# Keys and values of the prompt memory as split products in a decoder step on one core

## The reference

```python
def memory_kv(mem, g, wk, wv):
    m = rms_norm(mem, g)                       # (1, 256, 1024)
    k = (m @ wk).reshape(B, M, XA_HEADS, XA_HEAD_DIM)
    v = (m @ wv).reshape(B, M, XA_HEADS, XA_HEAD_DIM)
    return k, v                                # both are outputs, too

def mixing(x, ...):
    z = rms_norm(x, g) @ w_in
    ...
    y_pool, pool_state = multiscale_pool(u_pool, ...)
    c, conv_state = causal_conv(u_rnn, ...)
    hs, hT = rg_lru(c, ...)
    y_rnn = hs * gelu(u_gate)
    merged = concatenate([rms_norm(y_pool, g_pool), rms_norm(y_rnn, g_rnn)])
    return merged @ w_out                      # "x1" in the kernel
```

## Time and profile before

| what | value |
|---|---|
| median of the three runs | 1110.73 us (1109.42 to 1127.9) |
| the profiled execution | 1109.17 us, span 1107.4 us |
| TensorE busy | 1061.4 us, 96% of the span |
| VectorE, ScalarE, GpSimd busy | 748.3, 646.5, 262.8 us (68%, 58%, 24%) |
| chain of work that ended last | TensorE 90%, DMA 3%, VectorE 3%, ScalarE 2% |
| keys and values on that chain (line 1659) | 5% |
| mean granted TensorE clock | 0.982 of full speed |

### The profile page before, as it was taken

The page is one execution under the profiler, slowest core; times in us unless marked ns, Lnnn a source line. Parts: engine busy times, 40 slices in busy tenths (PEclk is TensorE's granted clock), DMA queues, the critical chain, the costliest instruction groups (busy, mean ns, idle before and its releaser), DMA issues.

```text
span 1107.4 us, 17623 instructions
## 1 busy us (share of the span) xinstructions
PE 1061.4 (96%) x5991; PEld 796.5 (72%) x5991; DVE 748.3 (68%) x1332; ACT 646.5 (58%) x850; POOL 262.8 (24%) x180
## 2 busy tenths in 40 slices
PE   5999999999999999999999999999999999999991
PEld 5999458999669888666667666766667666766660
DVE  4733834633934575787788777887788778887762
ACT  4374343432643313677767776677767776677662
POOL 1001320000000101233333333333333333333321
PEclk8999999999999899999999999999999999999996
DMA  9500336050953525899999999999999999999945
GB/s 300 225 4 31 142 143 229 1 229 27 379 211 157 227 79 192 288 359 375 368 367 369 368 377 363 351 357 357 364 366 369 359 356 358 369 367 374 361 113 172
DMA packets 64342, 299.02 MB, mean 270 GB/s; under 512 B 12591, under 2 KB 15227, under 8 KB 39718
## 3 DMA queue, kind: packets, MB, share of 16 engines
q1 hardware_dynamic: 49102, 261.93, 61.7%
q0 software_dynamic: 15200, 36.55, 13.4%
HBM read 281.34 MB, written 34.00 MB: 285 GB/s over the span
## 4 chain that ended last, share of the span: by engine, by line
PE 90%; DMA 3%; DVE 3%; ACT 2%; SPq 1%; issue 1%; POOLq 0%; ACTq 0%; DVEq 0%
PE pair L1920 23%; PE pair L181 18%; PE pair L1954 16%; PE pair L1933 10%; PE pair L1659 5%; PE pair L1905 5%; PE pair L1562 3%; PE pair L1940 1%; DMA regA<-in_w_in 1%; PE pS L1868 1%; PE pair L1752 1%; PE pair L1760 1%; PE pS L1731 1%; DMA acc_rows<-regL 1%; DMA regL<-h_rows,regL 1%; DVE regL L1113 1%
## 5 line engine op out<-in xcount | busy, mean ns | idle before, releaser
L1920 PE MATMUL pair<-w_hi,h_parts 128*96 128x512 f32 x768 | 267.7, 430 | 0.0
L715 POOL DMA_INDIRECT acc_rows<-regL x64 | 93.0, 1453 | 389.8 <-ACT regL L1032 275.2
L1920 PEld LDWEIGHTS pair<-w_hi,h_parts 128*96 128x96 f32 x768 | 121.5, 165 | 69.7 <-issue 33.9
L1954 PE MATMUL pair<-w_hi,act_parts 128*96 128x512 f32 x512 | 165.0, 404 | 2.6 <-DVE act_parts L1509 2.6
L706 POOL DMA_INDIRECT regL<-h_rows,regL x65 | 139.7, 2148 | 74.7 <-DVE regL L1351 49.4
L1032 ACT ACTIVATE regL<-pair,regL 96x1024 f32<-96x1024 f32 x64 | 71.1, 1110 | 125.0 <-PE pair L1954 125.0
L1455 DVE TENSOR_TENSOR lo_A<-regA,w_hi 128x1536 fp32r<-128x1536 f32 x64 | 111.9, 1749 | 0.2 <-ACT w_hi L992 0.2
L1954 PEld LDWEIGHTS pair<-w_hi,act_parts 128*96 128x96 f32 x512 | 80.2, 167 | 29.9 <-issue 2.8
L992 ACT CAST w_hi<-regA 128x1536 fp32r<-128x1536 f32 x64 | 94.7, 1482 | 0.0
L1505 DVE TENSOR_TENSOR lo_B<-regB,w_hi 128x2048 fp32r<-128x2048 f32 x32 | 73.4, 2293 | 29.6 <-ACT w_hi L1027 29.6
L1505 DVE TENSOR_TENSOR lo_A<-regA,w_hi 128x2048 fp32r<-128x2048 f32 x32 | 73.4, 2292 | 24.7 <-ACT w_hi L1027 24.7
(11 more groups left out here) (344 smaller groups left out, 2207.3 us busy)
## 6 DMA issues: line engine op xcount, KB each, us to landing
regA<-in_exp_w_gate SPq DMA_DIRECT2D x32, 1024.0 KB, 9.1
regA<-in_exp_w_up SPq DMA_DIRECT2D x32, 1024.0 KB, 12.2
regA<-in_exp_w_down SPq DMA_DIRECT2D x32, 1024.0 KB, 14.0
regB<-in_exp_w_down SPq DMA_DIRECT2D x32, 1024.0 KB, 15.3
regB<-in_exp_w_gate SPq DMA_DIRECT2D x16, 1024.0 KB, 10.0
regB<-in_exp_w_up SPq DMA_DIRECT2D x16, 1024.0 KB, 13.6
regC<-in_exp_w_gate SPq DMA_DIRECT2D x16, 1024.0 KB, 9.2
regC<-in_exp_w_up SPq DMA_DIRECT2D x16, 1024.0 KB, 12.6
```

The lines of the kernel that those rows point to most:

```text
L715: pool.indirect_dma_start(acc_rows, bass.IndirectOffsetOnAxis(ap=kept[0:SLOTS, r, 0:1].bitcast(U32), axis=0), yX[r][0:SLOTS, :], None, bou ...
L1920: ins = pe.matmul(out, x, w, start=False, stop=half == 1 and k == CUT_K - 1 and s == 2, skip_group_check=True)
L1954: ins = pe.matmul(pair[2][0:SLOTS, h, :], act_parts[:, x, k, :], w[:, k, cols], start=k == 0 and s == 0, stop=k == KF - 1 and s == 2)
```

## The change

The keys and values become split products. ScalarE's mT copies now write the rounded part (`mT_hi`), and VectorE, after its polynomial for softplus, makes the rest (`leave_mT`) and is now the one that sets the pair free. The weights of K and V are cut in chunks of 128 rows by 1024 columns: `cut_kv(n)` on ScalarE and `leave_kv(n)` on VectorE, n = 0 to 7 for K and 8 to 15 for V. Rounded parts rotate through five places for K and three for V (`KV_PLACE`), the rests overwrite the weights. `kv` goes over the chunks outermost and serves both token tiles with each, so K(0) and K(1), and V(0) and V(1), end together. The sums of squares and the spreading of `nbp` stand between the chunks of V, the turning of the keys stands behind `nbr`.

```diff
-    o += [(("mT", q), "act") for q in range(2)]
+    o += [(("mT", q), "dve") for q in range(2)]
...
-    o += [(("K", t), "act") for t in range(MT)] + [(("yp", g), "act") for g in range(KP)] + [(("V", 0), "act"), (("KT", 0), "act")]
-    o += [("nbp", "dve"), (("KT", 1), "act"), (("V", 1), "act"), ("nbr", "dve"), ("hl", "act")]
-    o += [(("x1", m), "dve") for m in range(KD)]
+    o += [(("K", t), "act") for t in range(MT)] + [(("yp", g), "act") for g in range(KP)] + [(("V", t), "act") for t in range(MT)]
+    o += [("nbp", "dve"), ("hl", "act"), ("nbr", "dve"), (("KT", 0), "act"), (("KT", 1), "act")]
+    o += [(("x1", 0), "dve", 2, 2)] + [(("x1", m), "dve") for m in range(1, KD)]
...
+        mT_hi, mT_lo = view(lo_A, 2048, KD, NMEM), view(lo_A, 0, KD, NMEM)
+        kv_parts = [view(lo_A, 4096 + D * j, D) for j in range(4)] + [kv_fifth[:, :]]
+        kv_hi = [kv_parts[j] for j in KV_PLACE]
+        kv_raw = [w[:, k, :] for w in (wk_v, wv_v) for k in range(KD)]
+        kv_lo = [view(lo, 0, KD, D)[:, k, :] for lo in (lo_B, lo_C) for k in range(KD)]
...
+            def cut_kv(n):
+
+                if n in (0, KD):
+                    a.wait_ge(wv_in if n else wk_in, 16)
+                earlier = [i for i in range(n) if KV_PLACE[i] == KV_PLACE[n]]
+                if earlier and earlier[-1] == KD - 1:
+                    a.wait_ge(made, J.no[("K", 1)] + 1)
+                elif earlier:
+                    a.wait_ge(kv_used, earlier[-1] + 1 - earlier[-1] // KD)
+                a.copy(kv_hi[n], kv_raw[n]).then_inc(kv_hi_made, 1)
...
-            take_kv("K", Kt, 0)
             for i in range(KP):
                 a.wait_ge(lru_m2, i + 1)
                 c.add(a.activation(rT[:, i, :], rT[:, i, :], ACT.Sqrt), lru_m)
+            take_kv("K", Kt, 0)
             take_kv("K", Kt, 1)
+            cut_kv(KD + 2)
...
+            for n in range(KD + 3, KD + 6):
+                cut_kv(n)
+            rooted(DP)
             for i in range(KP):
+                if i in (0, 2):
+                    cut_kv(KD + 6 + i // 2)
                 a.wait_ge(y_rnn, i + 1)
                 squared(rT[:, i, :], gT[:, i, :])
-            take_kv("V", Vt, 0)
-            rooted(DP)
-            take_kt(0)
             a.wait_ge(stored, 16 * 6)
             O.cut_hi(a, 0)
             O.cut_hi(a, 1)
             cut_norm(ytmp, KD, 0, KP)
             rooted(DP)
-            take_kt(1)
-            O.cut_hi(a, 2)
+            take_kv("V", Vt, 0)
             take_kv("V", Vt, 1)
-            cut_norm(ytmp, KD + KP, KP, KP)
             p = J.wait_made(a, "hl")
             J.take(a.copy(hlO[0:1 + DEC, :], pair[p][0:1 + DEC, 0, :]), "hl")
+            O.cut_hi(a, 2)
+            take_kt(0)
+            cut_norm(ytmp, KD + KP, KP, KP)
+            take_kt(1)
...
+            def leave_mT():
+
+                v.wait_ge(made, J.no[("mT", 1)] + 1)
+                for q in range(2):
+                    p = J.wait_made(v, ("mT", q))
+                    v.wait_ge(mt_hi, 4 * q + 4)
+                    for j in range(4):
+                        k = 4 * q + j
+                        cl = COL["norm_mem"] + k
+                        ins = v.scalar_tensor_tensor(mT_lo[:, k, :], pair[p][:, j // 2, (j % 2) * NMEM:(j % 2 + 1) * NMEM],
+                                                     par[:, cl:cl + 1], mT_hi[:, k, :].bitcast(F32), ALU.mult, ALU.subtract)
+                    J.take(ins, ("mT", q))
+
+            def leave_kv(n):
+                v.wait_ge(kv_hi_made, n + 1)
+                v.tensor_tensor(kv_lo[n], kv_raw[n], kv_hi[n].bitcast(F32), ALU.subtract).then_inc(kv_lo_made, 1)
...
                 if n == 2 * KP - 1:
                     softplus()
+                    leave_mT()
+                if n >= 2 * KP:
+                    leave_kv(n - 2 * KP)
+            leave_kv(4)
...
                 c.add(v.scalar_tensor_tensor(dT[:, g, :], dT[:, g, :], 1.0 / w, uP[:, g, PBUF:PBUF + NT],
                                              ALU.mult, ALU.subtract), d_ready)
+                if g:
+                    leave_kv(4 + g)
...
+            leave_kv(KD)
+            leave_kv(KD + 1)
             v.wait_ge(lru_m, KP)
             step(v.memset(rT[:, :, 0:1], 1.0))
...
-            def kv(what, w, t):
-                p = J.begin(pe, (what, t))
-                for k in range(KD):
-                    if what == "K" and t == 0:
+            def kv(what, first, ks):
+
+                if ks[0] == 0:
+                    for t in range(MT):
+                        kv_pair[t] = J.begin(pe, (what, t))
+                for k in ks:
+                    if what == "K":
                         J.wait_taken(pe, ("mT", k // 4))
-                    for h in range(2):
-                        ins = pe.matmul(pair[p][:, h, :], mT[:, k, t * P:(t + 1) * P], w[:, k, h * 512:(h + 1) * 512],
-                                        start=k == 0, stop=k == KD - 1)
-                J.made_by(ins)
+                    pe.wait_ge(kv_lo_made, first + k + 1)
+                    for t in range(MT):
+                        cols = slice(t * P, (t + 1) * P)
+                        for h in range(2):
+                            of = slice(h * 512, (h + 1) * 512)
+                            for i, (x, w) in enumerate(((mT_hi, kv_hi), (mT_lo, kv_hi), (mT_hi, kv_lo))):
+                                ins = pe.matmul(pair[kv_pair[t]][:, h, :], x[:, k, cols], w[first + k][:, of],
+                                                start=k == 0 and i == 0, stop=k == KD - 1 and i == 2)
+                        if k == KD - 1:
+                            J.made_by(ins)
+                    if k < KD - 1:
+                        ins.then_inc(kv_used, 1)
+
+            kv_pair = [0, 0]
...
-            pe.wait_ge(wk_in, 16)
-            for t in range(MT):
-                kv("K", wk_v, t)
+            kv("K", 0, range(KD))
 
             pe.wait_ge(plw_in, 16)
             for g in range(KP):
                 pe.wait_ge(d_ready, g + 1)
                 project(("yp", g), lambda k: plw[:, g, :], lambda k: dT[:, g, :], range(1))
-            pe.wait_ge(wv_in, 16)
-            kv("V", wv_v, 0)
+            kv("V", KD, range(0, 3))
             sum_squares(0, sqP, True, True, (group_added, KP - 1))
-            turn_keys(0)
+            kv("V", KD, range(3, 6))
             spread("nbp")
+            kv("V", KD, range(6, 7))
             sum_squares(0, rT, True, True, (group_added, 2 * (KP - 1)))
             seen["squares"] += 2 * KP
-            turn_keys(1)
-            kv("V", wv_v, 1)
-            spread("nbr")
+            kv("V", KD, range(7, KD))
             p = J.begin(pe, "hl")
             for i in range(KP):
                 ins = pe.transpose(pair[p][0:1 + DEC, 0, i * P:(i + 1) * P], cT[:, i, SEQ - 1:NT], ident[:, :])
             J.made_by(ins)
+            spread("nbr")
+            turn_keys(0)
+            turn_keys(1)
```

27 lines of the change are left out of this document (20 added, 7 removed).

## The result

The changed kernel took 1121.38, 1121.73, 1134.97 and 1135.2 us; their median is 1128.35. Beside it before took 1108.71 to 1110.73 us, and once 1127.9. The ratio is 1.017 (95%: 1.0135 to 1.0205). The forecast was 1118 us, the range 1111 to 1125: the change lost time, as forecast, but more than forecast, and in two groups that no part of the prediction explains. Seven more runs gave 1121.03 in the median (1120.2 to 1137.3) and a ratio of 1.0093 (1.0073 to 1.0114); that interval ends at some 1122 us and says nothing of the upper group. Of 13 runs in all, 8 lie at 1120 to 1122.5 us and 5 at 1134.6 to 1137.3, with 1121.7 in the middle. So how far the first median lies from the forecast is in part luck: two of those four runs fell into the upper group, and in all 13 it is five.

A forecast was written before the change was run, and what follows sets the result against it. TensorE, holding 90% of the chain, was taken as the bound. The terms -10.8 + 0.9 + 2.6 + 1.9 + 13.7 - 2.0 + 2.9 = +9.2 on 1109.17 gave 1118 us, range 1111 to 1125.

The forecast's parts named there:

- this 174.96: Start of x1 in the kernel before, in us, freed of 0.6 us of waiting; the change was priced by its shift.
- The low end: Small ends of the second to sixth terms with the large one of the products: 1113 us.
- Point 1: K and V products on TensorE: 192 float32r products at 0.230 us replace 54.9 us; -10.8 us (to -9.6).
- Point 2: Rests of mT: z's second of the last four tiles waits for VectorE's `leave_mT` to free the pair; +0.9 (0.5 to 1.5).
- Points 3 and 4: Cuts ahead of yp delay the copies of K, +2.6 (0.7 to 4); GpSimd's sums between V's chunks, +1.9 (0 to 2).
- Point 5: Behind V: norms, second root, V copies and `nbr` run one after another before x1; +13.7 us (11 to 15).
- KT -2.0: Turning of the keys, 2 x 1.02 us, now lies inside the stretch behind V; -2.0 us.
- Point 6: TensorE's clock falls to 0.50 after idling behind V and ahead of x1; +2.9 us (0 to 4).
- The sum: All terms together: +9.2 us on the profiled execution's 1109.17, giving 1118 us.
- V's chunks did not run dry: Rival: V's last five chunks each wait for their own copy and subtraction; 1121 to 1133 us, chance 0.14.
- the count bound: Forecast: first norm waits for V(1)'s end through `wait_made`; rival that it doesn't bind: 1112 to 1116 us, chance 0.13.
- nothing more was covered: Rival: all work behind V is covered and x1 starts when V ends; 1098 to 1104 us, chance 0.08.

The follow-up runs named there:

- experiments 2 and 3: Changed kernel with an own count for `nbp`: 1117.26 us, ratio 1.0088; changed kernel with x1's first product in KT(0)'s psum pair: 1115.21 us, ratio 1.0057.
- the profile at 1106.89: A later profile of the unedited kernel before, nothing changed; 1106.89 us, its loop 625.5 us.
- that at 1122.41: A later profile of the unedited changed kernel; 1122.41 us, its loop 630.1 us.
- the mended kernel: Changed kernel with own count for `nbp`, `nbp` applied before O's cuts, x1's first product in `nbp`'s pair, keys turned after x1's fourth product: 1108.7 us, ratio 0.9985.

## Why the prediction was wrong, point by point

- **The failing step** is in its first part: "What comes behind is the same program on the same chain, so the change is worth what it does to this 174.96". The program is the same; its pace isn't. In the unedited change the loop took 630.1 us in one profile and 642.8 to 646.6 in three, for 625.5 to 625.7 in the three of before, so 4.4 to 21 us were added behind the stage, by weights that land late and by the chain of scatters. The chain of before shows PE in the loop because PE came last there; the chain of scatters, where it holds the loop, is slower by only 0.3 us a block (10.22 for 9.93). I had not asked how far behind PE the next in line was. In the profiles of five edits of the change the loop lost 4 to 5 us; before with a delay lost 5.2 and 1.3 in its two profiles; with half of the scattered rows gone the loops of both kernels are alike. What sets the slower paces off stays open.
- **The low end** of 1113 was added up wrongly: the small ends of points 2 to 6 with the -9.6 of point 1 come to +0.6, 1110 us and not 1113.
- **Point 1** (-10.8): 192 products at 0.228 us are 43.8 for 54.9; with the short breaks at the sums between V's chunks it is 44.3, -10.6. Right.
- **Point 2** (+0.9): 1.1 of waiting, 1.4 in z as a whole. Right.
- **Points 3 and 4** (+2.6, +1.9): PE waited 0.7 + 0.4 for the yp products' pairs and 0.4 for the sum. From the first product of yp to V's first it took 5.3 us for 3.5, and the two sums took 3.3 for 2.5: +1.8 and +0.8, within the ranges given, but mis-sized, 2.6 for 4.5. The meeting of VectorE and GpSimd is real, though:

```profile
141.17 4.51 DVE L1273 TENSOR_TENSOR_SCAN regL<-regL 128x512 f32<-128x512 f32 x2
...
146.72 2.33 DVE L1273 TENSOR_TENSOR_SCAN regL<-regL 128x512 f32<-128x512 f32 x2
148.97 1.20 DVE L1226 TENSOR_TENSOR lo_C<-regC,lo_A 128x1024 fp32r<-128x1024 f32 x1
...
155.01 2.32 DVE L1226 TENSOR_TENSOR lo_C<-regC,kv_fifth 128x1024 fp32r<-128x1024 f32 x1
```

and GpSimd's sums beside them, for which the earlier trace rows has six in 8.25:

```profile
137.54 7.06 POOL L681 TENSOR_TENSOR regL<-regL 128x520 f32<-128x520 f32 x3 [16.40 <-ACT regL L764]
152.37 6.14 POOL L681 TENSOR_TENSOR regL<-regL 128x520 f32<-128x520 f32 x3 [7.76 <-ACT regL L764]
```

  Between 144.60 and 152.37 us GpSimd adds nothing. There a rest of 1024 columns takes 1.20 us and two scans 2.33; beside the additions they take 2.32 and 4.51, and GpSimd's three take 7.06 and 6.14 for the 4.1 of three undisturbed ones. Each operation that meets the other side is held up by 0.7 to 1.1 us. The Trainium skill (SBUF — State Buffer, SBUF: two separate sides) says that such operations of the two shut each other out for a whole instruction, and these rows agree. It cost little: no chunk of V waited for its rest, and GpSimd's additions began 1.3 us sooner, counted from z, than the 140.5 us at which point 4 put them.
- **Point 5** (+13.7, and KT -2.0): from V's end (162.68) to x1 17.6 us, forecast 15.8 and 1.3 for the clock. Each wait stood where it was said to be; experiments 2 and 3 take them away one by one. The small work at the low clock took about twice as long (`nbr` 2.62 us for 1.25), not half as long again.
- **Point 6** (+2.9): x1 is 1.6 us longer, as forecast, and the clock was at 0.50 for its first 4 us.
- **The sum** for the stage: +9.2 forecast, +9.1 measured. That it fits to the tenth is luck in part: points 3 and 4 were 1.9 us too high, the others together as much too low.
- **The rivals**: V's chunks did not run dry, the count bound, nothing more was covered. None of them was a loop behind that changes its pace, though the view of the transfers would have shown landings of 9.4 us at 550 and 22.5 at 910.

## What to carry to other kernels

A chain that shows one engine through a loop tells who comes last there, not by how much: before pricing a shift ahead of it, look at the landing times of the loop's loads over its length. If they grow, the loop lives on its lead, and its pace can differ from run to run of one and the same program: take several runs and several profiles before pricing an edit by one of them. To price a stage in such a kernel, take some load off the loop in both versions; the difference that is left comes near the stage's own.

## What the runs showed of the hardware

- A scatter-add of 96 rows landed after 7.6 us (median over the loop) where the weights kept up, 8.7 where they fell behind, 9.3 in the chained pace, with the same share of busy DMA engines, 1.02 (one stretch of 100 us of the profile at 1106.89, of that at 1122.41 and of the first profile of the change; columns as in the clock's rows above):

```profile
870.00:970.00 100.00, 100.00 (x493) 68.77 (x492) 80.75 (x110) 72.27 (x82) 36.78 (x21) 1.00 1.02 369
```

```profile
870.00:970.00 100.00, 97.58 (x470) 66.47 (x469) 75.97 (x107) 66.92 (x77) 37.20 (x20) 1.00 1.02 363
```

```profile
870.00:970.00 100.00, 97.31 (x468) 64.85 (x467) 78.07 (x107) 70.67 (x78) 33.83 (x20) 1.00 1.02 356
```

  So that share doesn't tell a loop that keeps up from one that falls behind; the GB/s do, barely, and the landing times plainly.
- The pace of the scatters can leave the chained state by itself: the mended kernel did after its fourteenth block, in the first profile of the change a scatter still waited for the landing ahead of it at 1058 us, in the 58th of 64 blocks.
